# Three edits to a two-block transformer kernel: v projected in quarters between q and k, an output product cut five heads to three, and an earlier reload of spilled tiles

## What is computed

```python
# first block
y_att = (o_att * silu(az)) @ w_br_att
y_dn = (o_dn * silu(dz)) @ w_br_dn
mix = (sigmoid(gate_att) * y_att + sigmoid(gate_dn) * y_dn) @ w_out
# second block, layers i = 0, 1
h = rms_norm(x, attn_norm[i])
q, k, v = split(h @ w_in[i], 3)                  # 1024 features each
if i == 0: o = stick_breaking_attention(q, k, v)  # 16 heads of 64
else:      o = differential_attention(...)        # 8 heads: two 64-wide maps, one 128-wide v, head norm
x = x + o @ w_out[i]
x = x + (silu(g @ w_gate[i]) * (g @ w_up[i])) @ w_down[i]   # g = rms_norm(x, ffn_norm[i]), 2816 wide
```

## Time and profile before

| | us |
|---|---|
| timed executions, median of 3 (lowest, highest) | 2290.36 (2289.06, 2294.2) |
| the profiled execution, its own time | 2294.88 |
| its span in the trace | 2292.6 |
| TensorE busy in it | 2198.6 |
| VectorE, ScalarE, GpSimd busy | 1194.4, 1009.2, 249.4 |
| mean granted TensorE clock | 0.988 |

### The profile page before, as it was taken

The page is one execution under the profiler, slowest core; times in us unless marked ns, Lnnn a source line. Parts: engine busy times, 40 slices in busy tenths (PEclk is TensorE's granted clock), DMA queues, the critical chain, the costliest instruction groups (busy, mean ns, idle before and its releaser), DMA issues.

```text
span 2292.6 us, 35315 instructions
## 1 busy us (share of the span) xinstructions
PE 2198.6 (96%) x14886; PEld 1693.3 (74%) x14886; DVE 1194.4 (52%) x2101; ACT 1009.2 (44%) x1919; POOL 249.4 (11%) x273
## 2 busy tenths in 40 slices
PE   6999999999999999899999999999999988999999
PEld 5776777777776877686656888888876556888887
DVE  5566666766644545532336543444557665443442
ACT  4565656656544236435544331333445444321331
POOL 0022221222120011102211000001001001000000
PEclk9999999999999999999999999999999989999999
DMA  4221221222115332121112232222221112322232
GB/s 169 79 89 61 66 75 53 81 83 84 56 49 175 105 129 92 56 71 41 37 37 73 98 102 86 101 98 92 74 74 55 36 38 65 102 92 92 93 103 79
DMA packets 34765, 185.77 MB, mean 81 GB/s; under 512 B 4000, under 2 KB 4384, under 8 KB 15408
## 3 DMA queue, kind: packets, MB, share of 16 engines
q1 hardware_dynamic: 34608, 183.53, 23.6%
HBM read 172.99 MB, written 7.90 MB: 79 GB/s over the span
## 4 chain that ended last, share of the span: by engine, by line
PE 86%; DVE 7%; ACT 3%; issue 2%; DMA 1%; POOL 0%; SPq 0%; POOLq 0%; DVEq 0%; ACTq 0%
PE ps L1557 84%; PE ps L1560 1%; ACT arena L2447 1%; DVE spl L1997 1%; DVE arena L2147 0%; DMA raw<-wstream 0%; ACT spl L2450 0%; DVE x L2324 0%; ACT arena L2450 0%; DVE hl L2292 0%; ACT hh L2447 0%; DMA on_t<-spill 0%; DVE arena L2141 0%; DVE arena L2186 0%; DVE x L2288 0%
## 5 line engine op out<-in xcount | busy, mean ns | idle before, releaser
L1557 PE MATMUL ps<-hh,spl 128*128 128x512 f32 x3232 | 1074.4, 405 | 32.3 <-DVE arena_r L2224 7.9
L1557 PEld LDWEIGHTS ps<-hh,spl 128*128 128x128 f32 x3232 | 607.2, 189 | 193.7 <-issue 45.7
L1557 PE MATMUL ps<-hl,spl 128*128 128x512 f32 x1552 | 628.4, 405 | 0.0
L1997 DVE TENSOR_TENSOR spl<-raw,spl 128x512 fp32r<-128x512 f32 x596 | 413.0, 719 | 173.3 <-ACT spl L2450 172.6
L1557 PE MATMUL ps<-arena_r,spl 128*128 128x512 f32 x1936 | 472.9, 399 | 10.7 <-DVE arena_r L2224 4.6
L1557 PEld LDWEIGHTS ps<-arena_r,spl 128*128 128x128 f32 x1936 | 364.8, 189 | 106.9 <-DVE arena_r L2228 7.1
L2450 ACT ACTIVATE spl<-raw 128x512 fp32r<-128x512 f32 x596 | 342.2, 618 | 142.3 <-PE ps L1557 141.1
L1557 PEld LDWEIGHTS ps<-hl,spl 128*128 128x128 f32 x1552 | 293.6, 189 | 71.6 <-issue 15.7
L1557 PE MATMUL ps<-arena 32*32 32x32 f32 (+7 forms) x5664 | 217.7, 225 | 14.7 <-DVE arena L2186 5.8
L2447 ACT ACTIVATE arena<-arena 128x512 f32<-128x512 f32 (+3 forms) x211 | 139.7, 663 | 191.6 <-DVE arena L2329 141.6
L1557 PEld LDWEIGHTS ps<-arena 32*32 32x32 f32 (+4 forms) x5664 | 126.7, 116 | 101.8 <-issue 76.1
(11 more groups left out here) (216 smaller groups left out, 1904.0 us busy)
## 6 DMA issues: line engine op xcount, KB each, us to landing
raw<-wstream SPq DMA_DIRECT2D x149, 1024.0 KB, 5.1
GS<-g_rows SPq DMA_DIRECT2D x16, 256.0 KB, 3.4
spill<-x SPq DMA_DIRECT2D x14, 256.0 KB, 2.8
arena<-spill SPq DMA_DIRECT2D x12, 256.0 KB, 5.0
arena<-arena SPq DMA_DIRECT2D x20, 128.0 KB, 2.9
on_t<-spill SPq DMA_DIRECT2D x10, 256.0 KB, 3.2
x<-xT SPq DMA_DIRECT2D x4, 512.0 KB, 7.1
spill<-arena SPq DMA_DIRECT2D x8, 256.0 KB, 2.1
```

The source lines that it names most:

```text
L1557: return pe.matmul(out, lhsT, rhs, start=start, stop=stop, skip_group_check=True)
L1997: tt(spl[:, p % 2, 1, c], raw[:, p % 2, c], spl[:, p % 2, 0, c].bitcast(F32), ALU.subtract) \
```

## The change

- **v in quarters.** The pair for quarter j of v is taken behind q and k of tile 0, 2, 4, 6 in layer 0, and of tile 1, 3, 5, 7 in layer 1 (`V_BEHIND`; `lay_out` follows).
- **Five heads, then three.** `out_proj` first adds heads 0 to 4, then 5 to 7 (`OUT_FIRST`). The splits no longer go to `hh`: those of layer 0 go to `pad`, `on_t` and four arena tiles, those of layer 1 to `GS`, `rv`, four arena tiles and, for head 7 alone, `hh[7]`. So the splits of layer 0 wait for nothing but their head, in layer 1 heads 4 to 7 also wait for the last `br_out` and head 7 for the last v quarter.
- **First branch's tiles staged apart.** The reload of `ya` uses arena tiles 26, 35 and 36 and starts behind `lv_q2` of head 7 and `on_b` of head 6; the reload of `yd` keeps the old tiles and starts behind `on_b` of head 7.

```diff
+OUT_FIRST = 5
+V_BEHIND = ((0, 2, 4, 6), (1, 3, 5, 7))
...
     def load_lane():
-        while ("on_b", 7) not in o.at or ("at_m", 7) not in o.at:
+        while ("lv_q2", 7) not in o.at or ("on_b", 6) not in o.at:
             yield
-        o.behind(o.at["on_b", 7], o.at["at_m", 7])
+        o.behind(o.at["lv_q2", 7], o.at["on_b", 6])
         o.now += 2.0
         for which in ("ya", "yd"):
+            while which == "yd" and ("on_b", 7) not in o.at:
+                yield
...
-            gemm(op, 4, first_done(m))
+            gemm(op, OUT_FIRST, first_done(m))
         for m in range(KT):
-            gemm(op, (4, 5, 6, 7), done(m))
+            gemm(op, range(OUT_FIRST, KT), done(m))
...
-        o.spawn("split", split_lane("oa", oa, m, [("st_out", m), ("st_k", 7)]))
+        o.spawn("split", split_lane("oa", oa, m, [("st_out", m)]))
...
-        if m == 0:
-            vproj(0)
+        if m in V_BEHIND[0]:
+            vproj(0, V_BEHIND[0].index(m))
...
-        o.spawn("split", split_lane("ob", ob, m, [("df_out", m), ("br_out", "k", 7)]))
+        behind = [("df_out", m)] + [("br_out", "k", 7)] * (m > 3) + [("v_out", 1, 3, 3)] * (m == 7)
+        o.spawn("split", split_lane("ob", ob, m, behind))
...
-        if m == 0:
-            vproj(1)
+        if m in V_BEHIND[1]:
+            vproj(1, V_BEHIND[1].index(m))
...
-        for name, ids in (("oa", (34, 35, 36, 37)), ("ob", (20, 21, 22, 39))):
-            HI[name + "_h"] = HI["hh"][0:4] + [R(i) for i in ids]
+        HI["oa_h"] = [pad_r[:, 0, :], pad_r[:, 1, :], on_r[:, 0, :], on_r[:, 1, :]] + [R(34 + k) for k in range(4)]
+        HI["ob_h"] = [GS_r[:, 0, :], GS_r[:, 1, :], rv_r[:, :]] + [R(i) for i in (39, 20, 21, 22)] + [HI["hh"][7]]
...
-        stage_of = [A(26), on_t[:, 0, :], on_t[:, 1, :]]
+        stage_of = {"ya": [A(26), A(35), A(36)], "yd": [A(26), on_t[:, 0, :], on_t[:, 1, :]]}
...
-                        for i in range(2):
-                            sp.wait_ge(sem(f"ua_out{i}"), 64)
+                        sp.wait_ge(sem("ar_out"), 10)
+                        sp.wait_ge(sem("on_b"), 7)
+                    if which == "ya":
+                        a = at["at_m", k]
+                        sp.wait_ge(sem(f"ua_out{a.i}"), 16 * a.out_n)
+                    if which == "yd" and k == 0:
                         sp.wait_ge(sem("on_out"), 128)
...
-            if m == 0:
-                tm(w, 2048, 4)
-        for k0, k1 in ((0, 4), (4, 8)):
+            if m in V_BEHIND[i]:
+                tm(w, 2048 + 256 * V_BEHIND[i].index(m), 1)
+        for k0, k1 in ((0, OUT_FIRST), (OUT_FIRST, 8)):
```

More of the change, by code:

```diff
@@ L737, in load_lane @@
     def load_lane():
-        while ("on_b", 7) not in o.at or ("at_m", 7) not in o.at:
+        while ("lv_q2", 7) not in o.at or ("on_b", 6) not in o.at:
             yield
-        o.behind(o.at["on_b", 7], o.at["at_m", 7])
+        o.behind(o.at["lv_q2", 7], o.at["on_b", 6])
         o.now += 2.0
         for which in ("ya", "yd"):
-            for k in range(KT):
+            while which == "yd" and ("on_b", 7) not in o.at:
+                yield
+            if which == "yd":
+                o.behind(o.at["on_b", 7])
+                o.now += 2.0
+            for k in range(KT):
+                while ("at_m", k) not in o.at:
+                    yield
+                if k == 7 and which == "ya":
+                    o.behind(o.at["at_m", 7])
+                    o.now += 2.0
                 while not stage_slots.ready():
@@ L958, in arrange, with vproj, done @@
     o.spawn("r2", r2_lane())
[L961 to L971, removed]
+    def vproj(layer, j):
+        if j == 0:
+            o.until(main.ready)
+            st = o.main("rs_col", layer, cost=[("PE", 0.4), ("AC", 0.3)])
+            st.u = main.take()
+            main.give(st.u)
+        def done(tb, u):
+            st = o.main("v_out", layer, tb, j, cost=[("AC" if tb % 2 else "DV", 0.4)])
+            st.u, st.tb, st.j, st.layer = u, tb, j, layer
+            main.give(u)
+        gemm_tok(h, done)
     def split_lane(name, op, k, ready):
@@ L1311, in build @@
         vec = sb("vec", [128, NVEC])
-        pad = sb("pad", [128, 2, S])
+        with nc.sbuf_tensor("pad", [128, 2, S], F32) as pad:
+            pass
+        pad_r = sb("pad_r", [128, 2, S], F32R)
         small = sb("small", [128, 600])
-        GS = sb("GS", [128, 2, S])
+        with nc.sbuf_tensor("GS", [128, 2, S], F32) as GS:
+            pass
+        GS_r = sb("GS_r", [128, 2, S], F32R)
         ident_r = sb("ident_r", [128, 128], F32R)
@@ L1320, in build @@
         arena_r = sb("arena_r", [128, NA, S], F32R)
-        on_t = sb("on_t", [128, 2, S])
+        with nc.sbuf_tensor("on_t", [128, 2, S], F32) as on_t:
+            pass
+        on_r = sb("on_r", [128, 2, S], F32R)
         st = sb("st", [128, 2, 2, 128])
         kdt = sb("kdt", [128, 2, 128])
-        rv = sb("rv", [128, 2, 2, 128])
+        with nc.sbuf_tensor("rv", [128, 2, 2, 128], F32) as rv:
+            pass
+        rv_r = sb("rv_r", [128, S], F32R)
         ps = ctx.enter_context(nc.psum_tensor("ps", [128, 8, S], F32))
@@ L1383, in build @@
         HI["yd_l"] = [R(17)] + [R(35 + k) for k in range(6)] + [R(8)]
-        for name, ids in (("oa", (34, 35, 36, 37)), ("ob", (20, 21, 22, 39))):
-            HI[name + "_h"] = HI["hh"][0:4] + [R(i) for i in ids]
+        HI["oa_h"] = [pad_r[:, 0, :], pad_r[:, 1, :], on_r[:, 0, :], on_r[:, 1, :]] + [R(34 + k) for k in range(4)]
+        HI["ob_h"] = [GS_r[:, 0, :], GS_r[:, 1, :], rv_r[:, :]] + [R(i) for i in (39, 20, 21, 22)] + [HI["hh"][7]]
+        for name in ("oa", "ob"):
             HI[name + "_l"] = [R(8 + k) for k in range(KT)]
@@ L1533, in sync @@
                     src = (spill if which == "ya" else spill2)[:, k, :]
-                    sp.dma_start(stage_of[q.i], src).then_inc(sem(f"re_ld{q.i}"), 16)
+                    sp.dma_start(stage_of[which][q.i], src).then_inc(sem(f"re_ld{q.i}"), 16)
                 elif q.kind == "load_x":
@@ L2226, in vector @@
                     which, k = q.key
+                    if which == "yd" and k == 0:
+                        w.wait_ge(sem("re_lo"), 8)
                     w.wait_ge(sem("re_hi"), q.n)
-                    tt(HI[which + "_l"][k], stage_of[q.i], HI[which + "_h"][k].bitcast(F32), ALU.subtract) \
+                    tt(HI[which + "_l"][k], stage_of[which][q.i], HI[which + "_h"][k].bitcast(F32), ALU.subtract) \
                         .then_inc(sem("re_lo"), 1)
@@ L2663, in scalar @@
                         empty(at["st_out", k].u)
-                        full(at["st_k", 7].u)
                     else:
                         w.wait_ge(sem("df_out"), at["df_out", k].n)
-                        w.wait_ge(sem("br_out"), 16)
+                        if k > 3:
+                            w.wait_ge(sem("br_out"), 16)
+                        if k == 7:
+                            full(at["v_out", 1, 3, 3].u)
                     copy(HI[name + "_h"][k], o8[k]).then_inc(sem("os_hi"), 1)
@@ L2671, in scalar @@
                     if q.n == 1:
+                        w.wait_ge(sem("sc_o"), 28)
+                        t = at["lv_q2", 7].u
+                        w.wait_ge(drained[t.b], t.n)
+                    if which == "yd" and k == 0:
                         w.wait_ge(sem("sc_o"), 32)
                     w.wait_ge(sem(f"re_ld{q.i}"), 16 * ((q.ld.n - 1) // 3 + 1))
-                    copy(HI[which + "_h"][k], stage_of[q.i]).then_inc(sem("re_hi"), 1)
+                    copy(HI[which + "_h"][k], stage_of[which][q.i]).then_inc(sem("re_hi"), 1)
                 elif kind == "eg_sig":
```

## The result

| | before | changed |
|---|---|---|
| timed executions, median (lowest to highest), us | 2290.21 (2289.06 to 2294.2) | 2254.03 (2252.9 to 2255.52) |
| the profiled execution, us | 2294.88 | 2254.5 |
| its span, us | 2292.6 | 2252.4 |
| TensorE busy, us | 2198.6 | 2182.1 |
| mean granted clock | 0.988 | 0.995 |

The ratio is 0.9834, with an interval of 0.9823 to 0.9846, which is 35 to 41 us. The ratio itself is worth 38 us, the two medians differ by 36.2; 30 were forecast.

What follows compares the result with a forecast made beforehand. TensorE, busy 2198.6 of 2292.6 us, was taken as the bound, so only its gaps and lowered clock could be won: 41.1 us off, 10.7 on, 30.4 less, from 2290.4 to 2260.0 us; range 2248 to 2279.

Steps and rivals of the forecast that it cites:

- Reload, 4.5 us: Start of ya: reload issued ahead of the last scan head's spill, so all 4.5 us go; bounds 3 and 4.5.
- Layer 0, 8.7 off: Layer 0's first output-product round: splits no longer wait for the last k; 8.7 us off, one 1 us gap left.
- switches: Stream matmuls behind transposes: 17 more return trips in layer 1, 4 fewer in layer 0, 0.09 us each; 1.1 us lost.
- Layer 1's attention, two thirds of 14.7 us: Layer 1's attention: VectorE's load at or below 76% of TensorE's cuts waits for `br_in`; 9.8 us off, bounds 3 and 14.7.
- Output product of layer 1, 18.1 us: Layer 1's output product: 11.1 us off from split waits and clock, 7.0 from the last head; bounds 12 and 18.1.
- the 11.1 of their term: Start of layer 1's output product: new buffers end the splits' wait for the last `br_out`; 11.1 us off with clock.
- The last head's 7.0 us: Layer 1's second round: starting after 40 blocks instead of 32 ends the wait for head 7; 7.0 us off.
- Second round, 5.8 us of gap a layer against 2.7: Output product's second round: 25.1 us chain against 19.3 us of TensorE work; 3.1 us a layer more gap than before.
- clock cost of 1.7 a layer: Second round of the output product: gaps this dense bring a lowered clock, adding 1.7 us a layer.
- the moved gaps: Rival: layer 1's VectorE backlog stays, waits for `br_in` appear elsewhere; 7.2 us less, 2283 us; chance 0.12.
- the v evictions: Rival: v's evictions queue behind attention; with 16 tiles hit 58 us lost, 2318 us; chance 0.04.
- the second rival: The second round is free and attention loses all its gaps: 45 us less, 2245.5 us; chance 0.14.

Runs made afterwards that it cites:

- v_one_piece: The changed kernel with all four pairs of v behind tile 0 again in both layers: 2281.42 us, ratio 0.9944 to the kernel before.
- late_splits: The changed kernel with no head split placed before the last k (layer 0) or last `br_out` (layer 1): 2272.9 us, ratio 0.9905 to the kernel before.
- four_four: The changed kernel with the output products cut four heads and four again: 2250.21 us, ratio 0.9811 to the kernel before.
- late_reload: The changed kernel with the reload of ya behind the last scan head's norm again, own staging tiles kept: 2262.73 us, ratio 0.9862 to the kernel before.
- six_two: The changed kernel with the output products cut six heads, then two: 2259.97 us, ratio 0.9855 to the kernel before.

## Why the prediction was right, point by point

- **Reload, 4.5 us: 6.1 to 6.4 by the traces, 6.4 and 6.7 by the ratios.** Right in mechanism, but above the term's bounds of 3 and 4.5. The term was taken from gaps, and part of the wait lies where the matmul still counts as busy.
- **Layer 0, 8.7 off with 4.8 on and 0.4 of switches off: 4.3 net; measured 3.7.** The number is right by errors that cancel, which is luck. The first round kept no gap (0.1 us, 1 expected) and the second cost no clock (1.7 expected), but 2.1 us of small gaps for ScalarE's passes came up under v, which I had priced at nothing.
- **Layer 1's attention, two thirds of 14.7 us: all but about 1 us of it.** This is the step that fell short. I kept a third since waits had begun at a load of 71 to 76% before; those loads were counted from the order of instructions. By the traces, VectorE's busy time over TensorE's, in each 16 blocks of the stream from 1728 on, was 81, 81, 65, 72, 68 and 79% (the last two are the ones I had at 82 and 92%), and the first wait stands at the end of the first of these, so the waits began at 81%, not at 71 to 76. In the changed kernel no 16 blocks before the output product are above 74%, and `br_in` holds TensorE for 0.5 us in all. `v_one_piece` shows that v's place did it; that the load is the reason is argued, not shown.
- **Output product of layer 1, 18.1 us: gone as forecast, but for another reason in part.** `late_splits` gives 10.6 us of layer 1 to the splits, near the 11.1 of their term. The last head's 7.0 us I credited to five and three; `four_four` has no such wait in layer 1, while `v_one_piece`, with five and three, waits 2.5 us. What brought the head forward there is v between the tiles, and five and three only bought 2.2 us of gap and some clock in layer 0. The reading of the earlier trace rows was also loose: 1898.4 is where the norm's last step starts, it ends at 1899.1, and the split is done 1.4 us later; the term does not use it.
- **Second round, 5.8 us of gap a layer against 2.7: 5.1 and 5.2 against 1.8 and 1.6.** The difference of 3.1 was measured as 3.3 and 3.6. Its clock cost of 1.7 a layer was wrong: the clock stayed at 1.00. No run shows the price of the switches, 1.1 us in all, by itself.
- **Sum, 30.4: 36.2.** By parts the forecast was 4.5 for the reload, 4.3 for layer 0 and 21.6 for layer 1 (9.8 + 11.1 + 7.0, less 4.8 for its second round and 1.5 for its switches); the stretches give 6.1, 3.7 and 27.6. The shortfall is mostly layer 1's: 4 us from the third of attention that I kept (14.7 less 9.8, of which about 1 stayed) and 1.7 from the clock of its second round. The time lay in the range. Of the rivals none came true as a whole: not the moved gaps (0.5 us left for `br_in`), not the v evictions (no wait for a bank of v is in the trace). Of the second rival one half did, attention without gaps, and the other half, a free second round, did not.

## What to carry to other kernels

Independent matmuls are cover: spread them over the stretch in which a latency chain (steps of other engines, each waiting for the last) runs beside them, and do not spend them ahead of it. Cutting a product so that its second round is shorter may save a wait for the last operand, but where a tile's chain on the other engines takes longer than its matmuls, every tile pays the difference; price that chain first, from `xo` to `xo`. And an edit that is bundled with a good one has to be timed alone: five and three cost about 4.5 us here inside a change that won 36.

## What the runs showed of the hardware that was not expected

- Where matmuls with a short wait each follow one another, the wait can show on the weight loads alone (0.78, 0.28 and 0.71 us in `late_reload`) and not as a gap of TensorE. Comparing the time between the same blocks of two traces found 1.6 us that the gaps did not.
- Gaps of 5.1 us in 26, most of it in five gaps of 0.4 to 1.5 us, left the clock at 1.00; in the kernel before, 5.8 us in 48 with gaps up to 2.0 us came with 0.89. In `six_two` five gaps of 1.5 us in a row, one every 3.2 us, left it at full speed as well. But in `late_splits`, layer 0, where no gap is over 1.5 us either, it was 0.97 in the stretch of 50 us. What sets these apart was not tested.
- A GpSimd addition of two SBUF tiles was itself lengthened, from 1.29 to 1.34 and 1.57 us, when VectorE's two-input instruction came first, by 0.56 and by 0.33 us.
